# Second mixer of a two-block network: another order of the work between the keys and the first attention steps

## The reference, cut to what matters

```python
def gqa_mixer(hc, hl, w_in, g_q, g_k, w_out, cos, sin, need_ctx):
    pl = hl @ w_in
    ql = gqa_q(pl[..., :GQA_Q_W], g_q, cos, sin, True)
    kl, vl = gqa_kv(pl[..., GQA_Q_W:], g_k, cos, sin, True)
    ...
    kc, vc = gqa_kv(hc @ w_in[:, GQA_Q_W:], g_k, cos, sin, False)
    ol = attention(ql, concat([kc, kl]), concat([vc, vl])) @ w_out
```

## Time and profile before

| | us |
|---|---|
| median of 3 runs | 2952.83 (2952.12 to 2958.28) |
| profiled execution | 2953.86 |
| its span | 2952.2 |
| PE busy in the span | 2749.4 (93%) |
| DVE busy | 1578.0 (53%) |
| ACT busy | 1018.4 (34%) |
| mean granted clock of PE | 0.967 of full speed |

### The profile page before, as it was taken

How to read it: one execution, slowest core, us unless ns; L and a number is a source line. 1 busy time by engine, 2 the same in 40 slices (tenths; PEclk the granted TensorE clock), 3 DMA queues, 4 the chain that set the end, 5 groups by cost and what they waited for, 6 DMA issues and landing times. The chain is left out here.

```text
span 2952.2 us, 35995 instructions
## 1 busy us (share of the span) xinstructions
PE 2749.4 (93%) x14526; PEld 2217.2 (75%) x14526; DVE 1578.0 (53%) x2342; ACT 1018.4 (34%) x1592; POOL 81.7 (3%) x108
## 2 busy tenths in 40 slices
PE   6979989999999978898999989899988999999997
PEld 3757877888888867777888866688856777777775
DVE  4568745333334365776444444355554666556566
ACT  2136533222222233554333333432233343333343
POOL 0110000000000000000000000000000000000000
PEclk9989999999999989999999999999998999999998
DMA  5430013233333311011222232222221222222221
GB/s 212 143 114 30 15 43 107 100 114 108 113 102 104 104 42 45 22 44 58 93 93 93 93 121 71 79 86 86 86 80 63 83 81 80 70 84 81 87 74 43
DMA packets 67242, 246.96 MB, mean 84 GB/s; under 512 B 7504, under 2 KB 7888, under 8 KB 66384
## 3 DMA queue, kind: packets, MB, share of 16 engines
q1 hardware_dynamic: 51280, 185.10, 18.6%
q0 software_dynamic: 14768, 55.51, 6.2%
q10 hardware_dynamic: 1040, 4.12, 0.4%
HBM read 242.45 MB, written 2.24 MB: 83 GB/s over the span
## 5 line engine op out<-in xcount | busy, mean ns | idle before, releaser
L2039 DVE TENSOR_TENSOR WL<-RAW,WH 128x1024 fp32r<-128x1024 f32 x331 | 405.1, 1225 | 680.5 <-ACT WH L1483 678.7
L718 PE MATMUL PS<-HM,WH 128*128 128x512 f32 x1752 | 707.8, 404 | 19.1 <-DVE HM L2046 10.9
L719 PE MATMUL PS<-HM,WH 128*128 128x512 f32 x1752 | 700.0, 400 | 0.0
L720 PE MATMUL PS<-HM,WL 128*128 128x512 f32 x1752 | 699.4, 399 | 0.0
L1483 ACT ACTIVATE WH<-RAW 128x1024 fp32r<-128x1024 f32 x331 | 349.8, 1057 | 822.8 <-PE PS L720 813.6
L718 PEld LDWEIGHTS PS<-HM,WH 128*128 128x128 f32 x1752 | 334.2, 191 | 95.4 <-issue 30.0
L720 PEld LDWEIGHTS PS<-HM,WL 128*128 128x128 f32 x1752 | 333.4, 190 | 80.2
L719 PEld LDWEIGHTS PS<-HM,WH 128*128 128x128 f32 x1752 | 334.1, 191 | 55.8
L718 PE MATMUL PS<-GM,WH 128*128 128x512 f32 x468 | 187.1, 400 | 4.3 <-DVE GM L2046 3.7
L719 PE MATMUL PS<-GM,WH 128*128 128x512 f32 x468 | 186.9, 399 | 0.0
L720 PE MATMUL PS<-GM,WL 128*128 128x512 f32 x468 | 186.9, 399 | 0.0
(11 more groups left out here) (377 smaller groups left out, 4615.0 us busy)
## 6 DMA issues: line engine op xcount, KB each, us to landing
RAW<-in_tiles SPq DMA_DIRECT2D x333, 512.0 KB, 3.3
MRAW<-in_mods POOLq DMA_DIRECT2D x80, 512.0 KB, 4.8
TB<-bias_rows POOLq DMA_DIRECT2D x16, 576.0 KB, 6.3
FIRST<-in_mods SPq DMA_DIRECT2D x8, 1024.0 KB, 23.2
X_M<-in_x ACTq DMA_DIRECT2D x1, 2048.0 KB, 16.2
VN_GB<-in_gm_rows POOLq DMA_DIRECT2D x2, 1024.0 KB, 5.7
out_x<-X_M SPq DMA_DIRECT2D x8, 256.0 KB, 2.0
X_C<-in_ctx ACTq DMA_DIRECT2D x1, 1024.0 KB, 19.2
```

The costliest lines, as they stand in the source:

```text
L718: pe.matmul(out_, wh, xh, start=first, stop=False, skip_group_check=True)
L719: pe.matmul(out_, wh, xl, start=False, stop=False, skip_group_check=True)
L720: return pe.matmul(out_, wl, xh, start=False, stop=last, skip_group_check=True)
L2039: dve.tensor_tensor(WL[:, s.mod(2), :], RAW[:, s.mod(2), :], f32(WH[:, s.mod(2), :]), ALU.subtract).then_inc(tile_split[s.mod(2)], 1)
```

## The change

On TensorE the sums of the first two queries move from behind value step 0 into its middle; the second key's spread moves behind all of query 0's projection; the scores of steps 0 and 1 move in front of value step 2; and in step 0 of the loop the transposes move in front of the first piece of the next projection. On ScalarE the copies of key 1 move behind the split of the second value tile, the first query's high half moves in front of the first values' (with a wait for value step 0 of its own), the exponentials of steps 0 and 1 in front of the last values' copy, and the splits of gqa_q+2 and gqa_q+3 behind them, the latter into step 0 of the loop. On VectorE `key_rope` becomes two functions, `key_turned` (the rotation) and `key_low` (the low halves): key 0's rotation moves in front of the split of query 1's tile, its low halves behind key 1's diagonal; the split of the first value tile moves in front of key 1's norm; key 1's low halves move behind the second value tile's split; and the last values' low half and the splits of gqa_q+2 and gqa_q+3 move into step 0 of the loop.

```diff
--- before.py
+++ after.py
@@ -1124,6 +1124,8 @@
 
                 pe.wait_ge(*((gqa_v_read, 1) if step == 2 else (query_read, step + 1)))
                 for n in range(2):
+                    if step == 0 and n == 1:
+                        query_sums(0)
                     x = token_chunk(2 * step + n)
                     o = v_bank(step)[:, n * 2 * P:(n + 1) * 2 * P].rearrange("p (v n) -> p v n", v=2)
                     for k in range(KC):
@@ -1204,23 +1206,23 @@
 
             project(0, 0, 9)
             key_sums(1)
-            project(0, 9, 18)
+            project(0, 9, 24)
             key_scales(1)
-            project(0, 18, 24)
             project(1)
             tile_ready(s + 4)
             tile_ready(s + 5)
             v_step(0)
-            query_sums(0)
             v_step(1)
-            v_step(2)
             scores(0)
             scores(1)
+            v_step(2)
             for w in range(GQA_UNITS):
                 pair, n = w // 8, w % 8
                 j = 2 * pair + 2
                 if w + 2 < GQA_UNITS:
                     scores(w + 2)
+                if w == 0:
+                    transposes(0)
                 if pair < 3:
                     if n == 0:
                         project(j, 0, 10)
@@ -1234,7 +1236,8 @@
                         project(j + 1, 15, 24)
                 elif n:
                     out_part(n - 1)
-                transposes(w)
+                if w:
+                    transposes(w)
                 if w >= 2 and w % 2 == 0:
                     values((w - 1) // 2)
                 if pair < 3 and n == 2:
@@ -1771,6 +1774,8 @@
                 if j < 2:
                     split(At(TILES["gqa_q"] + j))
                     act.wait_ge(head_sum, j + 1)
+                    if j:
+                        key_high(1)
                 else:
                     act.wait_ge(rope_done, 10 + j)
                 act.activation(SQ[:, j % 2, TC:TA], q_bank(j), ACT.Square).then_inc(query_sq, 1)
@@ -1779,6 +1784,8 @@
                     split(At(TILES["gqa_q"] + j + 2))
 
             def query_high(j):
+                if j == 0:
+                    act.wait_ge(gqa_v_done, 1)
                 act.wait_ge(rope_done, 12 + j)
                 copy(QG[j // 2 % 2][0][:, j % 2, :], RG[0][:, :]).then_inc(query_hi, 1)
 
@@ -1824,24 +1831,24 @@
 
             key_high(0)
             query_taken(0)
-            key_high(1)
             query_taken(1)
-            v_taken(0)
             query_high(0)
             root_of_queries(0)
+            v_taken(0)
             query_high(1)
             v_taken(1)
-            v_taken(2)
-            for j in range(2):
-                split(At(TILES["gqa_q"] + 2 + j))
             exps(0)
             exps(1)
+            split(At(TILES["gqa_q"] + 2), (gqa_v_done, 3))
+            v_taken(2)
             for w in range(GQA_UNITS):
                 pair, n = w // 8, w % 8
                 j = 2 * pair + 2
                 pt_high_of(w)
                 if w + 2 < GQA_UNITS:
                     exps(w + 2)
+                if w == 0:
+                    split(At(TILES["gqa_q"] + 3))
                 if w >= 2 and w % 2 == 0:
                     out_high((w - 1) // 2)
                 if pair < 3:
@@ -2490,11 +2497,13 @@
                 dve.scalar_tensor_tensor(out=HEADN[:, n, TC:TA], in0=HEADN[:, n, TC:TA], scalar=gk, in1=PS[:, 4, :], op0=ALU.mult, op1=ALU.mult
                                          ).then_inc(head_inverse, 1)
 
-            def key_rope(n):
+            def key_turned(n):
                 dve.wait_ge(head_inverse, 2 * n + 2)
                 if n:
                     dve.wait_ge(key_ready, n)
                 rope(At(9 + n), slice(0, P), HEADN[:, n, TC:TA], RG[0][:, :], rope_done, ROPE_TG, RG)
+
+            def key_low(n):
                 dve.wait_ge(key_hi, n + 1)
                 low(KG[1][:, n, 0:TC], HEADN[:, n, 0:TC], KG[0][:, n, 0:TC])
                 low(KG[1][:, n, TC:TA], RG[0][:, :], KG[0][:, n, TC:TA]).then_inc(key_ready, 1)
@@ -2580,19 +2589,21 @@
             split(s + 2)
             key_scale(0)
             key_norm(0)
+            key_turned(0)
             split(s + 3)
-            key_rope(0)
             key_scale(1)
+            key_low(0)
+            split(s + 4)
             key_norm(1)
-            split(s + 4)
-            key_rope(1)
-            dve.wait_ge(key_ready, 2)
+            key_turned(1)
+            dve.wait_ge(rope_done, 11)
             gq = COLS[:, COL["gq"]:COL["gq"] + 1]
             dve.stream_shuffle(LN[:, 2, 16:17], gq, SWAP).then_inc(rope_gain, 1)
             dve.tensor_scalar(ROPE_TG[:, 0, :], ROPE_TG[:, 0, :], gq, None, ALU.mult).then_inc(rope_gain, 1)
             dve.wait_ge(rope_gain, 1)
             dve.tensor_scalar(ROPE_TG[:, 1, :], ROPE_TG[:, 1, :], LN[:, 2, 16:17], None, ALU.mult).then_inc(rope_gain, 1)
             split(s + 5)
+            key_low(1)
             query_parts(0)
             query_turned(0)
             query_low(0)
@@ -2602,9 +2613,6 @@
             scale_of_queries(0)
             query_low(1)
             v_read(1)
-            v_read(2)
-            for j in range(2):
-                split(At(TILES["gqa_q"] + 2 + j))
             maximum(0)
             maximum(1)
             prob(0)
@@ -2613,11 +2621,16 @@
                 j = 2 * pair + 2
                 if w + 1 < GQA_UNITS:
                     prob(w + 1)
+                if w == 0:
+                    split(At(TILES["gqa_q"] + 2))
                 if w + 2 < GQA_UNITS:
                     maximum(w + 2)
                 if pair == 3 and n:
                     part_added(n - 1)
                 pt_low(w)
+                if w == 0:
+                    v_read(2)
+                    split(At(TILES["gqa_q"] + 3))
                 if w >= 2 and w % 2 == 0:
                     out_low((w - 1) // 2)
                 if pair < 3:
```

## The result

The changed kernel takes 2936.84 us (median of 5 runs, 2935.23 to 2940.14), the kernel before 2952.12 us in the same comparison (5 runs, 2949.36 to 2958.28). The ratio is 0.9947, with a 95% interval of 0.9937 to 0.9958: 15.6 us faster, between 12.4 and 18.6. I had forecast 13.0 us and 2939.8 us, with a range from 2936.5 to 2944.5. The range was drawn too high and too narrow, and the experiments were to say why.

A forecast was written before the change was run, and what follows sets the result against it. TensorE, busy 93% of the span, was taken as the bound, so only its idle or half-clock time counts; 5.6 + 1.25 + 1.3 + 3.25 + 1.6 = 13.0 us gave 2939.8 us, range 2936.5 to 2944.5.

The forecast's parts named there:

- The key's spread: Hole before the second key's spread: 4.1 us idle and 1.5 us of slow clock go, 5.6 us in all.
- The value tiles: Hole before the first value step shrinks from 3.71 to 2.45 us, the bare copy and subtraction chain: 1.25 us.
- The clock behind it: After the remaining 2.45 us hole before the first value step, TensorE's clock does not fall: 1.3 us.
- rival 1: The clock does fall behind the 2.45 us hole: 11.7 us gained, 2941.1 us; chance 0.30.
- The clock behind the other two: Half-clock stretches behind the holes at the key's spread and the scores of step 2 go: 1.5 and 1.6 us.
- The softmax's start: Hole before the scores of step 2 goes from 4.10 to 0.85 us: 3.25 us, plus 1.6 us of clock.
- Steps 0 and 1 at nothing: VectorE's added read and two splits in the loop's first steps cost nothing; uncovered, at most 3.2 us.
- The query sums: 16 matmuls moved into the middle of value step 0, not removed; covered by 2.8 us, so no gain or loss.
- From the sum to the time: Whole kernel: the 13.0 us sum, taken from the median of 2952.83 us, gives 2939.8 us.
- the spread of the runs: Allowance at the range's low end: two missing slow stretches give 2937 us, with this spread 2936.5.

The follow-up runs named there:

- the part alone: Under the key's spread: kernel before with only key 0's rotation and the spread moved, ratio 0.9971; under the softmax: only scores, exponentials and transposes moved, 0.9973.
- the second part alone: Kernel before with only the second value tile's split moved ahead of key 1's low halves on VectorE and key 1's copies on ScalarE: ratio 0.9991.

## Why the prediction was right, and where it was wrong

- **The key's spread, 5.6 us:** right. The hole of 4.09 us is gone and the part alone shortens the stage by 4.1 and 6.2 us, against the two executions of before. The diagonal was 0.2 us ahead of the last six matmuls of query 0 and 1.6 us ahead of the spread (forecast 1.5). That these six matmuls were needed as cover was wrong: undone, the spread still doesn't wait.
- **The value tiles, 1.25 us:** right, 3.71 to 2.45 us, in all five traces with this chain. VectorE was 0.81 us ahead in the four with the changed order and 0.68 us in the second part alone.
- **The clock behind it, 1.3 us: this step failed.** "I take no fall, as the work in front of this hole is dense." It fell in all of the traces that have this hole (the changed kernel twice, the second part alone, the sums and the transposes undone), and behind 2.83 us too; the term is 0 instead of 1.3 us. What I took for the distinguishing mark, dense work in front, is none. That was my rival 1, which I gave 0.30; its sum, 11.7 us, is what the stage shows in the first pair of traces: 11.8. The Trainium skill ("TensorE: Matmul & The Clock Gate", "HAM oscillation — how this bites in real kernels") puts the fall down to idle gaps of the engine. The traces agree that filling the gap keeps the clock, but the gaps that the section tells of are waits for transfers that are longer than the products between them, and this one is a short hole in dense work, so it did not settle the case. Nor does the length settle it here: the hole of 2.47 us near 1880 stands in all fourteen traces, and in thirteen the clock behind it stayed at 1.00.
- **The clock behind the other two, 1.5 and 1.6 us:** right for one execution and too small for another. Filling all three holes of the kernel before is worth 4.2 us against its first trace (forecast 4.4 with the 1.3) and 6.4 us against its second, whose stretches behind the first and third hole are 6.8 us instead of 3.4. I had priced them by a single trace.
- **The softmax's start, 3.25 and 1.6 us:** right. 4.10 to 0.71 us is 3.39; with the clock 4.7 us in the part alone.
- **Steps 0 and 1 at nothing:** right. The low part of step 1 ended 0.15 us ahead of TensorE's turn. That the slack was almost nil shows with the transposes undone: 0.82 us of waiting at once. The transposes' move was worth 1.4 us, more than the 0.6 of TensorE's time that I gave it.
- **The query sums, nothing:** right.
- **From the sum to the time: this step failed too, and it is what put the time at the range's end.** The clock's 1.3 us alone would have made the kernel slower than forecast, not faster. The median is lower by 15.3 us, the stage by 11.8 in the same pair of executions. In that pair of traces the quick start accounts for the 3.5 us between them: the changed kernel's trace had it, 3.45 us at the first matmul of the mixers, and the kernel before has it too in another execution. How much of the medians' difference it makes is not shown, as only one execution of each comparison was traced: against the second trace of the kernel before the stage alone gives 13.9 us. I had allowed 0.5 us for "the spread of the runs"; the traces show 4.0 us between the two starts, and medians of five runs over them differed by 3.8 us for one and the same kernel (2936.84 and 2940.65). The changed kernel's ten runs have their median at 2938.1 us, 1.7 below the forecast. That 13.0 us stands between 11.8 and 13.9 is in part luck: a clock term that is not there makes up for two that were priced low.

What remains open: why TensorE's clock is full in some executions and half in others between 24 and 33 us, and why it falls behind the one hole of some 2.5 us each time and behind another of the same length almost never. No run varied either.

## What to carry to other kernels

Look for the holes of the bottleneck engine one by one and ask which single instruction ends each; then move it ahead of whatever its engine does between having its inputs and getting to it. A hole costs its length and often a slow start behind it: here the last microsecond, from 2.45 to 1.49 us, took the slow start away and was worth more than the 1.25 us before it. Whether the clock falls is not to be read from the length alone, so look at the granted clock behind each hole, in more than one trace. And with some microseconds at stake in three thousand, compare a stage in the trace rather than the whole time: the stage here repeated within 0.03 us when its slow stretches were the same (and differed by 2.1 us when they were not), the median of the whole time within 4.

## What the runs showed of the hardware that I had not expected

- Executions of one kernel have two kinds of start: groups of four small matmuls (L839) between 24 and 33 us take 0.61 or 1.01 us, and the first matmul of the mixers comes at 56.7 to 58.0 or at 61.0 to 62.2 us.
- Behind the hole of 2.45 us the granted clock fell to 0.50 in five traces of five, and behind that of 1.49 us in none of two. But behind the hole of 2.47 us near 1880 it fell in one of fourteen, and behind three holes of 1.88 us near 270, 318 and 364, which the change does not touch, in 14 of 42. One of these, in the kernel before:

```profile
318.52 1.22 PE L968 MATMUL PS<-IDENT,PROB 128*128 128x128 f32 x6 [1.88 <-DVE PTA L2046]
```

```profile
318.90:322.10 3.20, 3.20 (x18) 3.20 (x17) 2.54 (x5) 2.27 (x6) 0.00 (x0) 0.50 0.00 0
```

- The slow stretch behind a hole of the stage lasted 3.4 or 6.8 us, and began anywhere from 2.2 us before the work started again to 1.5 us after it. It changed between two executions of the kernel before, and with it the stage by 2.1 us.
- Cutting a subtraction of 1024 columns in two costs VectorE only 0.06 us (1.29 against 1.23).
